# Start addresses of the matmul operands in SBUF: staying activations at a multiple of 128 bytes, moving operands 32 bytes behind one

## The reference

```python
def first_block(x, ...):                       # depth 1
    h = rmsnorm(x, norm_mix_g[l])
    proj = einsum('bsd,dc->bsc', h, w_in[l])   # 7 x 1024 columns: u, v, bg, cg, xs, ga, gb
    v = rmsnorm(gelu(v), norm_v_g[l])
    a = spatial_gating(gelu(u), v, w_s[l], b_s[l])
    c = bg * causal_dwconv(cg * xs, conv_w[l])
    m = sigmoid(ga) * (a @ w_proj_a[l]) + sigmoid(gb) * (c @ w_proj_b[l])
    x = x + m @ w_out[l]
    z = relu(rmsnorm(x, norm_ff_g[l]) @ w_ff1[l])          # 4096 columns
    x = x + (z * z) @ w_ff2[l]
    return rmsnorm(x, norm_final_g)

def second_block(x, ...):                      # depth 2
    # layer 0: differential attention, 8 heads; layer 1: latent attention, 16 heads
    # each followed by: x = x + conv_ffn(rms_norm(x, g)), hidden width 2816
    #   u = h @ w_up;  c = causal depthwise conv(u) + b;  g, val = split(c)
    #   (silu(g) * val) @ w_down
    # and one more rms_norm at the very end
```

## The kernel before, in words

| tensor | before | after |
|---|---|---|
| `whl`, staying (in `columns`, L823, L825) | 0 | 0 |
| `whl`, moving in `v_rows`, `rows`, `down_tokens` | 0 | 32 |
| `whl`, moving in `value_rows` | 0 | 0 |
| `hT`, moving (in `columns`, L823, L825) | 32 | 32 |
| `hT`, staying in `v_rows` | 32 | 32 |
| `hT`, staying in `rows` | 32 | 0 |
| `lat`/`zT`, moving | 32 | 32 |
| `zT`, staying in `down_tokens` | 32 | 0 |
| `lat`, staying in `value_rows` | 32 | 32 |
| `mT`, `aT`, `cT`, moving | 32 | 32 |
| `raw`, `xT` | 0 | 0 |
| `const` (identity and tables) | 32 | 64 |
| `ones` | 32 | 64 |
| `ss`, `std`, `rstd`, `t_act`, `t_dve`, `conv_in` | 0 | 32 |
| `conv_out` | 32 | 64 |
| `hf`, `q_sb`, `k_sb`, `v_sb`, `prob`, `attn`, `attnT`, `vtok`, `wsT` | 32 | 32 |

## Time and profile before

### The profile page before, as it was taken

How to read it: one execution, slowest core, us unless ns; L and a number is a source line. 1 busy time by engine, 2 the same in 40 slices (tenths; PEclk the granted TensorE clock), 3 DMA queues, 4 the chain that set the end, 5 groups by cost and what they waited for, 6 DMA issues and landing times.

```text
span 1024.9 us, 18891 instructions
## 1 busy us (share of the span) xinstructions
PE 1008.6 (98%) x7284; PEld 943.4 (92%) x7284; DVE 755.2 (74%) x1007; ACT 592.5 (58%) x833; POOL 6.6 (1%) x20
## 2 busy tenths in 40 slices
PE   7999999999999999999999999999999999999997
PEld 6999999999999999977899999999999998888886
DVE  6576655457776656787879877777886688888886
ACT  7554565655544435657867555555646675666665
POOL 0000000000000000000000000000020000000000
PEclk9999999999999999999999999999999999999999
DMA  8635656556666564354464666674425474666652
GB/s 299 210 108 194 208 176 206 192 164 190 198 199 194 188 210 175 130 202 137 164 191 124 187 188 192 187 209 129 135 58 137 125 213 139 201 191 193 189 167 82
DMA packets 191264, 178.86 MB, mean 175 GB/s; under 512 B 17444, under 2 KB 169586, under 8 KB 191218
## 3 DMA queue, kind: packets, MB, share of 16 engines
q1 hardware_dynamic: 191218, 178.22, 56.1%
HBM read 177.15 MB, written 1.05 MB: 174 GB/s over the span
## 4 chain that ended last, share of the span: by engine, by line
PE 83%; DVE 6%; ACT 5%; DMA 4%; issue 2%; SPq 0%; ACTq 0%; DVEq 0%
PE psum L621 15%; PE psum L623 15%; PE psum L622 15%; PE psum L823 13%; PE psum L825 7%; PE psum L628 4%; PE psum L630 4%; PE psum L629 4%; ACT whl L1268 3%; DVE whl L1753 2%; DMA raw<-w_in 2%; DMA raw<-da_w_qkv 1%; PE psum L971 1%; PE psum L955 1%; PE psum L970 1%
## 5 line engine op out<-in xcount | busy, mean ns | idle before, releaser
L1753 DVE TENSOR_TENSOR whl<-raw,whl 128x2048 fp32r<-128x2048 f32 (+2 forms) x145 | 298.3, 2062 | 89.0 <-ACT whl L1268 88.6
L1268 ACT ACTIVATE whl<-raw 128x2048 fp32r<-128x2048 f32 (+2 forms) x145 | 248.7, 1718 | 85.2 <-DMA raw<-w_in 32.6
L621 PE MATMUL psum<-hT,whl 128*128 128x256 f32 (+1 forms) x784 | 219.9, 281 | 1.6 <-DVE hT L1828 1.0
L623 PE MATMUL psum<-hT,whl 128*128 128x256 f32 (+1 forms) x784 | 218.9, 279 | 0.0
L622 PE MATMUL psum<-hT,whl 128*128 128x256 f32 (+1 forms) x784 | 218.8, 279 | 0.0
L823 PE MATMUL psum<-hT,whl 128*128 128x512 f32 x608 | 212.9, 391 | 0.0
L825 PE MATMUL psum<-hT,whl 128*128 128x256 f32 x608 | 171.4, 282 | 0.0
L621 PEld LDWEIGHTS psum<-hT,whl 128*128 128x128 f32 (+1 forms) x784 | 147.1, 188 | 2.4 <-DVE whl L1753 0.9
L622 PEld LDWEIGHTS psum<-hT,whl 128*128 128x128 f32 (+1 forms) x784 | 147.1, 188 | 0.1
L623 PEld LDWEIGHTS psum<-hT,whl 128*128 128x128 f32 (+1 forms) x784 | 147.1, 188 | 0.0
L621 PE MATMUL psum<-lat,whl 128*128 128x256 f32 (+1 forms) x512 | 144.0, 281 | 0.0
(11 more groups left out here) (254 smaller groups left out, 1628.3 us busy)
## 6 DMA issues: line engine op xcount, KB each, us to landing
raw<-w_ff SPq DMA_DIRECT2D x32, 1024.0 KB, 5.7
raw<-w_in SPq DMA_DIRECT2D x24, 1024.0 KB, 5.2
raw<-ffn_w_up SPq DMA_DIRECT2D x44, 512.0 KB, 4.9
q_sb<-ffn_w_up SPq DMA_DIRECT2D x44, 512.0 KB, 5.0
raw<-da_w_qkv SPq DMA_DIRECT2D x12, 1024.0 KB, 5.1
q_sb<-ffn_w_down SPq DMA_DIRECT2D x22, 512.0 KB, 3.7
raw<-ffn_w_down SPq DMA_DIRECT2D x22, 512.0 KB, 3.8
raw<-w_proj_a SPq DMA_DIRECT2D x4, 1024.0 KB, 5.4
```

The lines of the kernel that those rows point to most:

```text
L621: mm(dst, weight(n, 0, cols, kt, c0, m), hi, start=start, stop=False, skip_group_check=True)
L623: return mm(dst, weight(n, 1, cols, kt, c0, m), hi, start=False, stop=stop, skip_group_check=True)
L1268: fn(whl[:, slot, 0, 0:w], landing(n)[:, 0:w], ACT.Copy).then_inc(hi_ready, 1)
L1753: tt(whl[:, slot, 1, 0:w], landing(n)[:, 0:w], whl[:, slot, 0, 0:w].bitcast(F32), ALU.subtract).then_inc(lo_ready, 1)
```

## The change

Three edits of addresses; no instruction is added, removed or moved on any engine, and the sequence of instructions (kinds, shapes and order) is the same for all five.

1. A slot of `whl` has 32 words (128 bytes) more per part. The new helper `parts(n, k, a, b)` gives the columns of chunk n; for the chunks of `v_rows`, `rows` and `down_tokens` they begin 8 words (32 bytes) into the slot, for all others at its start. ScalarE and VectorE write, and TensorE reads, through it.
2. `hT` gets 8 words more: the tile is seen either from word 8 (`hT`, as before 32 bytes behind a multiple of 128) or from word 0 (`h_rows`, a multiple of 128). `h_rows` holds the activations of the stage `rows` alone (`round_x`, `rest_x`). `lat` gets 24 words more, and `z_staying` is the same four tiles 24 words (96 bytes) further on, at a multiple of 128; it is used by the last feed-forward stage.
3. The two fillers `half_line` and `half_line_m` are replaced by one of 16 words behind `lat`, by which all that follows up to `r_da` moves to another remainder (table above).

```diff
-        whl = sb("whl", [P, RING, 2, SLOT], F32R)
+        w_space = sb("whl", [P, RING, 2, SLOT + 32], F32R)
         xT = sb("xT", [P, KT, SEQ])
-        sb("half_line", [P, 8])
-        hT = sb("hT", [P, KT, 2, SEQ], F32R)
+        LINE, HALF_LINE = 32, 8
+        h_space = sb("hT", [P, KT * 2 * SEQ + HALF_LINE], F32R)
+        hT, h_rows = [h_space[:, at:at + KT * 2 * SEQ].rearrange("p (k h s) -> p k h s", h=2, s=SEQ)
+                      for at in (HALF_LINE, 0)]
         hf = sb("hf", [P, KT, SEQ])
-        lat = sb("lat", [P, 5, 2, SEQ], F32R)
-        zT = lat[:, 0:4, :, :].rearrange("p (a b) h s -> p a b h s", a=2)
+        l_space = sb("lat", [P, 5 * 2 * SEQ + LINE - HALF_LINE], F32R)
+        lat = l_space[:, 0:5 * 2 * SEQ].rearrange("p (k h s) -> p k h s", h=2, s=SEQ)
+        z_moving, z_staying = [l_space[:, at:at + 4 * 2 * SEQ].rearrange("p (a b h s) -> p a b h s", a=2, h=2, s=SEQ)
+                               for at in (0, LINE - HALF_LINE)]
+        sb("half_line", [P, LINE // 2])
...
-        sb("half_line_m", [P, 8])
...
+        def parts(n, k, a, b):
+
+            at = 8 if n < N_MIX or N_DA <= n < N_WO or N_FFN1 <= n and is_down(n - N_FFN1) else 0
+            return w_space[:, n % RING, k, at + a:at + b]
...
             def weight(n, part, cols, kt, c0, m):
-                return whl[:, n % RING, part, kt * cols + c0:kt * cols + c0 + m]
+                return parts(n, part, kt * cols + c0, kt * cols + c0 + m)
...
-                    z = zT[:, q, late_z(l, j, units), :, :]
+                    z = z_staying[:, q, late_z(l, j, units), :, :]
...
-                    last = tokens(flat(rows_bank(step, t)), n, w_hi, w_lo, hi_lo(hT, kt), t, kt == 0, kt == KT - 1)
+                    last = tokens(flat(rows_bank(step, t)), n, w_hi, w_lo, hi_lo(h_rows, kt), t, kt == 0, kt == KT - 1)
...
-                fn(whl[:, slot, 0, 0:w], landing(n)[:, 0:w], ACT.Copy).then_inc(hi_ready, 1)
+                fn(parts(n, 0, 0, w), landing(n)[:, 0:w], ACT.Copy).then_inc(hi_ready, 1)
...
-            def round_x(c, gain):
+            def round_x(c, gain, h=hT):
 
                 for kt in (2 * c, 2 * c + 1):
-                    fn(hT[:, kt, 0, :], xT[:, kt, :], ACT.Identity, scale=gain(kt)).then_inc(h_hi, 1)
+                    fn(h[:, kt, 0, :], xT[:, kt, :], ACT.Identity, scale=gain(kt)).then_inc(h_hi, 1)
...
             def ffn(l, n0, units, k, gain=None):
                 f = ffs[l]
+                zT = z_staying if l == 2 else z_moving
...
-                        round_x(c, gain)
+                        round_x(c, gain, h_rows if k + 1 == QKV else hT)
...
-                tt(whl[:, slot, 1, 0:w], landing(n)[:, 0:w], whl[:, slot, 0, 0:w].bitcast(F32),
+                tt(parts(n, 1, 0, w), landing(n)[:, 0:w], parts(n, 0, 0, w).bitcast(F32),
                    ALU.subtract).then_inc(lo_ready, 1)
```

More of the change, by code:

```diff
@@ L865, in down_unit @@
                         for kt in range(kts):
-                            z = zT[:, q, kt + late_z(l, j, units), :, :]
+                            z = z_moving[:, q, kt + late_z(l, j, units), :, :]
                             last = columns(bank[blk // 2][:, blk % 2, :], n, D, kt, blk * P, P,
@@ L1139, in value_rows @@
                 for kt in range(2):
-                    w_hi, w_lo = [whl[:, n % RING, part, kt * D:(kt + 1) * D].rearrange(
+                    w_hi, w_lo = [parts(n, part, kt * D, (kt + 1) * D).rearrange(
                         "p (h s e) -> p h s e", s=2, e=MLA_V)[:, :, 1, :] for part in range(2)]
@@ L1263, in split_hi @@
                     return
-                slot, w = n % RING, chunk_words(n)
+                w = chunk_words(n)
                 act.wait_ge(landed[raw_slot(n)], i * landed_per_pass(n) + landed_count(n))
@@ L1289, in split_hi_half @@
                 cols = slice(half * SLOT // 2, (half + 1) * SLOT // 2)
-                fn(whl[:, n, 0, cols], landing(n)[:, cols], ACT.Copy).then_inc(half_hi if half == 0 else hi_ready, 1)
+                fn(parts(n, 0, cols.start, cols.stop), landing(n)[:, cols], ACT.Copy).then_inc(half_hi if half == 0 else hi_ready, 1)
             def round_h(kt):
@@ L1814, in split_lo_half @@
                 cols = slice(half * SLOT // 2, (half + 1) * SLOT // 2)
-                tt(whl[:, n, 1, cols], landing(n)[:, cols], whl[:, n, 0, cols].bitcast(F32),
+                tt(parts(n, 1, cols.start, cols.stop), landing(n)[:, cols], parts(n, 0, cols.start, cols.stop).bitcast(F32),
                    ALU.subtract).then_inc(half_lo if half == 0 else lo_ready, 1)
@@ L1824, in rest_x @@
             def rest_x(k, c, gain):
+                h = h_rows if k == QKV else hT
                 for kt in (2 * c, 2 * c + 1):
                     dve.wait_ge(h_hi, KT * k + kt + 1)
-                    stt(hT[:, kt, 1, :], xT[:, kt, :], gain(kt), hT[:, kt, 0, :].bitcast(F32), ALU.mult,
+                    stt(h[:, kt, 1, :], xT[:, kt, :], gain(kt), h[:, kt, 0, :].bitcast(F32), ALU.mult,
                         ALU.subtract).then_inc(h_ready, 1)
```

## The result

| | before | after |
|---|---|---|
| median (runs) | 1026.87 us (6) | 1034.20 us (6) |
| lowest to highest | 1026.09 to 1028.04 | 1034.02 to 1035.65 |
| profiled execution, its span | 1026.7, 1024.9 us | 1034.25, 1032.5 us |

The ratio is 1.0071 (1.0062 to 1.0081): the change makes the kernel 7.3 us slower. The forecast was 1024.0 us, and its range ended at 1027.1.

A forecast was written before the change was run, and what follows sets the result against it. TensorE's own stream was taken to set the pace. Gains of 2.4 us (`rows`, `down_tokens`) and 0.15 us (slow pairs), rounded to 2.5 us, gave 1024.0 us against the 1026.48 us median; 8-in-10 range 1020.9 to 1027.1 us.

The forecast's parts named there:

- `value_rows`, and all of `columns`, L823 and L825: Matmuls said to keep their address remainders under the change; effect nothing.
- 233.4 − 229 = 4.4 ns each, 552 × 4.4 = 2.4 us: `rows` and `down_tokens`, both operands changing place, (32, 0) to (0, 32): priced from L823, 2.4 us off.
- A: The forecast: the pair (0, 32) is worth to `tokens` what L823 shows; 1024.0 us, chance 0.47.
- rival B: Addresses don't matter; L823's 4.4 ns come from its two banks or mixed widths; 1026.5 us, chance 0.30.
- `v_rows` … I take nothing, and keep −1.0 to +1.9 us: `v_rows`, 96 matmuls, only moving weights change, (32, 0) to (32, 32): no comparable row, so nothing, with that range.
- the reading I had announced: `v_rows` decides the cause: staying at 233.3 ns means the staying operand counts, falling means the moving one.
- The three slow pairs behind each down unit: First three wide pairs after a down unit, 353 ns not 347: 0.3 us if the lag goes, half taken, 0.15 us.
- Plain float32, VectorE and ScalarE: Plain float32 matmuls and transposes, VectorE and ScalarE operands: many starts move by 32 bytes; for both engines, nothing.
- Rival C: Faster outcome of 1020.9 us, the range's low end; its claim is not in the text given; chance 0.10.
- Rival D: The moving operand wants to start at a multiple of 128, so the kernel slows by 2.9 us: 1029.4 us, chance 0.13.
- if `columns` moves at all: Sign that the prediction is wrong: any change in the distances between `columns` matmuls, as outside `tokens` none should change.
- A's own range: The forecast's narrower range: 1023.3 us with `v_rows` gaining, to 1024.9 us at 3.1 ns per matmul.

The follow-up runs named there:

- the second probe: Kernel before plus, behind its last result, its own three matmul patterns at all 64 pairs of starts in 32-byte steps; `columns` 113.3 to 120.2 ns.
- The change with the harm taken out: Changed kernel with slots 256 bytes longer instead of 128 and tensors behind `lat` 128 bytes on; 1027.34 us, ratio 0.9995 to the kernel before.
- the first probe: Kernel before plus, behind its last result, streams repeating one float32r matmul at chosen pairs of starts; 256 columns 113.3 to 120.0 ns per matmul.

## Why the prediction was wrong

1. **"`value_rows`, and all of `columns`, L823 and L825: their remainders don't change. Nothing."** This step failed, and it alone accounts for the result: `columns` lost 8.7 us. The remainders were taken modulo 128, and the cost repeats with 256 (slots longer by 128 bytes: 119.0 ns; by 256: 116.7). The diff had it in plain sight: 32 words more per part shift every second part by half of 256. For the wide form the step held (+0.2 us in 1216 matmuls), though L825's low weights went from (128, 160) to (0, 160) as well: the second probe has 346 to 347 ns for the wide pattern at both pairs.
2. **"233.4 − 229 = 4.4 ns each, 552 × 4.4 = 2.4 us".** This term failed too. In a stream of its own the pair (0, 32) costs 233.4 ns for 512 columns, what (32, 0) cost. L823's 229 belongs to its mixture with L825: the wide pattern had 346 to 347 ns a pair at every pair of addresses 32 apart. The change with the harm taken out measured 0.9995, a gain of nothing, where A said −2.5 us. So rival B was right about the price, "the 4.4 ns are then due to the two banks that L823 writes or to the mixture of widths", while its heading, "the addresses don't matter", is wrong: `tokens` runs from 226.6 to about 235 ns by its addresses. Of its two causes the banks don't exist: `up_sums[q][:, b]` is one of the eight pieces of 2 × 256 words of `psum`, 512 adjacent words, just as the destination of `tokens` is. What is left is the mixture, L823 and L825 in turn; no run takes them apart.
3. **"`v_rows` … I take nothing, and keep −1.0 to +1.9 us".** Right in size: 231.1 ns, 2.2 less, 0.2 us in 96 matmuls. Its low weights start at 32 modulo 256 here; with both parts at 160 it gained 6.4 ns, 0.6 us. But the reading I had announced, "if it falls [it is] the moving one" that counts, is too simple: it is the pair. No run shows the −1.0 and the +1.9 us: in the runs above `v_rows` is at 226.9 to 233.3 ns, a gain of 0.6 us to nothing. Two streams with the same remainder are not in one another's way at 512 columns, where such pairs are the best (226.9 to 229.4 ns in the kernel); at 256 columns the first probe has 119.9 to 120.0 ns for them, among the slowest of its table.
4. **"The three slow pairs behind each down unit"**, 0.15 us: about right, and too small to matter. Over the 18 down units the three take 1051 ns on average after and 1056 before, 0.1 us in all. That they depend on how `tokens` stands, as this term supposed, shows in the changed kernel with slots of whole 256 bytes and in the one with all at 160, where they take 1043.
5. **Plain float32, VectorE and ScalarE: nothing.** These held: the busy times of VectorE and ScalarE moved by 2.1 us or less, and no group of plain float32 matmuls became slower (32 matmuls of 128 columns are 111.5 ns from start to start in both places, before and after). That the profiled execution lost 7.6 us and not 8.7 comes from the waits at its start (the transposes above), which the forecast did not have. The six matmuls of 256 columns that take 1.29 us don't all have one remainder: two read `conv_out`, which starts at 32, and four `t_dve`, which starts at 0. The price is the same, 215 to 216 ns from start to start.
6. **Rival C**, whose 1020.9 us is the low end of the range, needs 5.6 us off, 10.1 ns in each of 552 matmuls. No run shows that term: with 512 columns and the staying tile at 0 or 128 the streams go with 226.6 to about 235 ns, never lower. **Rival D** had the right sign and the wrong place: the matmuls of `tokens` lost 0.3 us in all, not 2.9, and a moving operand 32 bytes behind a multiple of 128 gives 226.9 ns when the staying one is there too.
7. **The test "if `columns` moves at all"** was the right one to write down, and the first view after, the mixer's timeline, answered it.
8. **A's own range**, "1023.3 … to 1024.9", is loosely added up: from 1024.0, `v_rows` gaining 1.0 us or 96 × 4.4 ns = 0.4 us gives 1023.0 or 1023.6, and 3.1 ns gives 1024.6 to 1024.8. Nothing hangs on it.

**What stays open.** The runs show that the two starts together, each modulo 256, set the cost. Why is not shown. By line, in the kernel after the slow step is that of the low matmul itself (120.6 ns), while the weights loaded next are high ones, 32 bytes from the moving operand. Nor is it shown why differences of 64 and of 32 have two rhythms or what puts a stream into one. Nor do I have a rule that gives each of the 64 values.

## What to carry to other kernels

When a change shifts addresses, write down both operands' starts for every kind of matmul, part by part, modulo at least twice the size that the change speaks of; a table with too small a modulus hides exactly the edit that costs. A price read off a matmul in a mixed stream (other widths between) does not carry to the same width and addresses in a stream of its own (229 ns against 233.4 here): where there is no such row, the range has to hold that. And count the matmuls on each side first: 1.8 ns on 4848 outweigh 4.4 ns on 552.

## What the runs showed of the hardware that I had not expected

- The cost of a float32r matmul in a stream depends on the pair of starts modulo 256: 113.3 to 120.2 ns for 256 columns, 226.6 to about 235 for 512, over starts in steps of 32 bytes. A slot stride off by 128 bytes costs this kernel 0.78%.
- For 512 columns with activations staying, equal starts are best, once the stream has settled: 226.9 to 229.4 ns against 233 in the kernel, 0.23% of the whole.
- A stream can keep to one of two rhythms at one and the same pair of addresses: `columns` at 117.8 or 116.7 ns at a difference of 32 bytes, at 117.8 or 113.3 at a difference of 64, where the kernel's time spreads over 11 us. A single profile of such a kernel (1020.7 us was profiled, 1024.6 is the median) says little.
